# Layer-norm roots taken with a token to a partition, and the router's logits and ranks, in a two-block transformer

## What is computed

```python
def layer_norm_2(x, g, b):
    mu = jnp.mean(xf, -1, keepdims=True)
    var = jnp.mean(jnp.square(xf - mu), -1, keepdims=True)
    return ((xf - mu) * lax.rsqrt(var + LN_EPS)).astype(x.dtype) * g + b

def routed_moe(x, router_w, router_b, w_gate, w_up, w_down):
    aff = jax.nn.sigmoid((xt @ router_w).astype(jnp.float32))      # 256 tokens x 16 experts
    sel = aff + router_b
    # best of 4 groups of 4 experts by the sum of its two best sel; in it the two best experts
    # weights: their aff, divided by the sum of both
    ...
for l in range(2):
    x = layer_norm_2(ALPHA * x + mixer(x), ln_g[l, 0], ln_b[l, 0])
    x = layer_norm_2(ALPHA * x + routed_moe(x, ...), ln_g[l, 1], ln_b[l, 1])
```

## Time and profile before

| | |
|---|---|
| median of 3 runs | 2592.41 us (2579.9 to 2612.1) |
| the profiled execution | 2592.51 us |
| its span, first to last instruction | 2590.7 us |
| mean granted TensorE clock over the span | 0.953 of full |

### The profile page before, as it was taken

One profiled execution on the slowest core, in us unless ns is written; L12 is line 12 of the kernel. 1 busy time (PEld: TensorE's weight loads), 2 busy tenths in 40 slices (PEclk: granted clock), 3 DMA queues, 4 the chain that ended last, 5 costly groups with the idle time before them and its releaser, 6 DMA issues.

```text
span 2590.7 us, 34009 instructions
## 1 busy us (share of the span) xinstructions
PE 2452.1 (95%) x14244; PEld 2102.6 (81%) x14244; DVE 1719.2 (66%) x2263; ACT 1194.5 (46%) x1520; POOL 98.7 (4%) x187
## 2 busy tenths in 40 slices
PE   5999999899999999999999998989999899899998
PEld 1788888767789999998899997867777787778776
DVE  5897776652656656655556655568878775688786
ACT  3222212333434444445444444456656644566665
POOL 0111111010000000000000000000000000000000
PEclk8999999998869999999899998999999896999999
DMA  6677887322114554455334452238877630388774
GB/s 257 216 243 255 267 265 260 131 76 95 66 35 161 179 195 163 175 193 217 139 131 164 178 203 99 82 128 332 333 270 297 252 114 33 114 330 321 287 301 181
DMA packets 80387, 501.19 MB, mean 193 GB/s; under 512 B 9604, under 2 KB 10708, under 8 KB 28496
## 3 DMA queue, kind: packets, MB, share of 16 engines
q1 hardware_dynamic: 59120, 423.66, 44.4%
q0 software_dynamic: 21088, 75.01, 9.1%
HBM read 497.58 MB, written 1.05 MB: 192 GB/s over the span
## 4 chain that ended last, share of the span: by engine, by line
PE 69%; DVE 16%; ACT 9%; issue 3%; DMA 2%; DVEq 0%; ACTq 0%; SPq 0%; POOL 0%; POOLq 0%
PE bank L394 67%; DVE wl L1913 7%; ACT wh L1304 6%; DVE macc L1949 2%; ACT s L1394 1%; DVE f L2074 1%; PE bank L577 1%; DMA raw<-in_wstream 1%; DVE s L2065 1%; DMA raw<-in_wmod 1%; PE bank L1198 1%; DVE rs L1973 1%; DVE hl L2049 1%; ACT H L1403 0%; DVE tmp L2042 0%
## 5 line engine op out<-in xcount | busy, mean ns | idle before, releaser
L1913 DVE TENSOR_TENSOR wl<-raw,wh 128x2048 fp32r<-128x2048 f32 (+1 forms) x430 | 903.8, 2107 | 404.7 <-ACT wh L1304 402.1
L1304 ACT ACTIVATE wh<-raw 128x2048 fp32r<-128x2048 f32 (+1 forms) x430 | 755.0, 1763 | 366.4 <-PE bank L394 354.3
L394 PE MATMUL bank<-hh,wh 128*128 128x258 f32 (+2 forms) x2200 | 700.8, 319 | 43.9 <-DVE wl L1913 23.5
L394 PE MATMUL bank<-hh,wl 128*128 128x258 f32 (+2 forms) x2200 | 681.5, 310 | 0.0
L394 PE MATMUL bank<-hl,wh 128*128 128x258 f32 (+2 forms) x2200 | 680.1, 309 | 0.0
L394 PEld LDWEIGHTS bank<-hh,wh 128*128 128x128 f32 x2200 | 428.1, 195 | 72.3 <-issue 23.0
L394 PEld LDWEIGHTS bank<-hl,wh 128*128 128x128 f32 x2200 | 429.0, 195 | 18.5
L394 PEld LDWEIGHTS bank<-hh,wl 128*128 128x128 f32 x2200 | 427.4, 194 | 19.2
L394 PE MATMUL bank<-wh,hh 128*128 128x512 f32 (+1 forms) x704 | 278.4, 395 | 5.5 <-DVE hl L2825 2.8
L394 PE MATMUL bank<-wl,hh 128*128 128x512 f32 (+1 forms) x704 | 274.0, 389 | 0.0
L394 PE MATMUL bank<-wh,hl 128*128 128x512 f32 (+1 forms) x704 | 274.0, 389 | 0.0
(11 more groups left out here) (424 smaller groups left out, 2716.8 us busy)
## 6 DMA issues: line engine op xcount, KB each, us to landing
raw<-in_wstream SPq DMA_DIRECT2D x393, 1024.0 KB, 5.0
mring<-in_wmod POOLq DMA_DIRECT2D x128, 512.0 KB, 4.6
raw<-in_wmod SPq DMA_DIRECT2D x8, 1024.0 KB, 9.1
X<-in_xT SPq DMA_DIRECT2D x1, 2048.0 KB, 12.3
bias<-in_nabias POOLq DMA_DIRECT2D x16, 128.0 KB, 2.5
c_sglg<-in_sglg POOLq DMA_DIRECT2D x1, 1024.0 KB, 5.2
c_sglb<-in_sglb POOLq DMA_DIRECT2D x1, 1024.0 KB, 7.5
out<-X SPq DMA_DIRECT2D x4, 256.0 KB, 2.2
```

The lines of the kernel that those rows point to most:

```text
L394: return e.matmul(out, lhsT, rhs, start=start, stop=stop, skip_group_check=True)
L1304: e.activation(wh[i % NB][:, o], raw[i % NR][:, o], ACT.Copy).then_inc(*slab_high(st.split + m))
L1913: e.tensor_tensor(wl[i % NB][:, o], raw[i % NR][:, o], wh[i % NB][:, o].bitcast(F32), ALU.subtract).then_inc(*slab_low(st.split + m))
```

## The change

1. Layer norms: the squares are summed with the squares as the stationary operand and one column of `ones` as the moving one: 16 products of one column, which leave a token's sum in its own partition, 128 x 2. Scale and epsilon, square root and reciprocal then work on 128 x 2. VectorE multiplies the identity by the roots (128 x 256 into `rs`), and one more product of `ones` with this diagonal spreads them to all partitions in PSUM, from where the scaling reads them.
2. For layer norms 0 and 2 ScalarE loads the table of the sigmoid by a small activation right behind the square root.
3. Router: `X` is now the stationary operand and the router's weights (16 columns) the moving one: 16 products, two a chunk. The logits come out as 128 x 32; the two transposes and the copy fall away.
4. Ranks: TensorE waits for "group" instead of "gates". VectorE does the weights of the experts behind the ranks, the flag and the two `Pm` tiles of group 0; the other six `Pm` tiles are written two at a time inside groups 0 to 2, behind the copy of the gates' values (`gG`).

```diff
         def layer_norm(i):
             st.kept.remove(bank_of["sum", i])
-            square_sums(7 + i, T)
+            b = bank(("ssq", 7 + i), dve_out, "mean", 7 + i)
+            for k in range(KC):
+                w.wait_ge(act_out, "square", 7 + i, k)
+                for c in range(2):
+                    ins = mm(b[:, c:c + 1], sq4[:, k % 4, P * c:P * c + P], ones[:, 0:1], k == 0 and c == 0, k == KC - 1)
+                ins.then_inc(*result("ssq", 7 + i, k))
+            b = bank(("ln root", i), dve_out, "scaled", 7 + i, KC - 1)
+            w.wait_ge(dve_out, "diag", 7 + i)
+            mm(b[:, 0:T], ones[:], rs[:, 0:T], True, True).then_inc(*result("ln root", i))
...
-                ins = mm(b[0:16, 0:T], q.rw[:, k, :], X[:, k, 0:T], k == 0, k == KC - 1)
+                for s_ in range(2):
+                    ins = mm(b[:, 16 * s_:16 * s_ + 16], X[:, k, P * s_:P * s_ + P], q.rw[:, k, :], k == 0 and s_ == 0, k == KC - 1)
             ins.then_inc(*result("aff", l))
-            b = bank(("aff t", l), dve_out, "aff t", l)
-            w.wait_ge(act_out, "aff", l)
-            for s_ in range(2):
-                ins = e.transpose(b[:, 16 * s_:16 * s_ + 16], q.rows[:, P * s_:P * s_ + P], ident[0:16, 0:16])
-            ins.then_inc(*result("aff t", l))
...
-            w.wait_ge(dve_out, "gates", l)
+            w.wait_ge(dve_out, "group", l)
...
-            root(7 + i, T)
+            w.wait_ge(dve_out, "mean", 7 + i)
+            e.activation(rt[:, 0:2], rt[:, 0:2], ACT.Sqrt).then_inc(*act_out("root", 7 + i))
+            if i % 2 == 0:
+                act(warm[:], ones[:, 0:1], ACT.Sigmoid, key=("sigmoid", i))
...
-            inv_root(7 + i, T, 1.0 / D, 1e-5)
+            e.tensor_scalar(rt[:, 0:2], banks[bank_of["ssq", 7 + i]][:, 0:2], 1.0 / D, 1e-5, ALU.mult, ALU.add).then_inc(*dve_out("mean", 7 + i))
+            w.wait_ge(act_out, "root", 7 + i)
+            e.reciprocal(rt[:, 0:2], rt[:, 0:2]).then_inc(*dve_out("inverse", 7 + i))
+            e.tensor_tensor(rs[:, 0:T].rearrange("p (b t) -> p b t", b=2), bc(ident[:], 2), rt[:, 0:2].unsqueeze(2).to_broadcast([P, 2, P]),
+                            ALU.mult).then_inc(*dve_out("diag", 7 + i))
...
+            places(0)
+            behind()
+            step(e.memset(q.top[:, :, 2:8], -4 * BIG), "two")
...
                 e.tensor_copy(q.gG[:, 0:S, :], banks[bank_of["ge", l, g]][:, 0:4 * S].rearrange("p (s x) -> p s x", x=4)).then_inc(*dve_out("ge", l, g))
+                if g < 3:
+                    places(g + 1)
```

More of the change, by code:

```diff
@@ L156, in program @@
     rs = sb(ctx, "rs", [P, 512])
+    rt = sb(ctx, "rt", [P, 4])
     sq4 = sq[:].rearrange("p a (b t) -> p (a b) t", t=T)
@@ L294, in moe_room @@
             q.top = sb(ph, f"top{l}", [P, 2, 8])
-            q.rows = sb(ph, f"aff{l}", [16, T])
             q.sm = sb(ph, f"sm{l}", [P, 8, 2])
@@ L678, in layer_norm @@
             st.kept.remove(bank_of["sum", i])
-            square_sums(7 + i, T)
+            b = bank(("ssq", 7 + i), dve_out, "mean", 7 + i)
+            w.wait_ge(dve_out, "ones")
+            for k in range(KC):
[6 more added lines that the diff above has]
+            mm(b[:, 0:T], ones[:], rs[:, 0:T], True, True).then_inc(*result("ln root", i))
         def mixer0():
@@ L1167, in group @@
                 b = small(("ge", l, g), dve_out, "ge", l, g)
+                w.wait_ge(dve_out, "gates", l)
                 for s_, c in blocks:
@@ L1801, in moe @@
             w.wait_ge(result, *before)
-            e.activation(q.rows[:], banks[bank_of["aff", l]][0:16, 0:T], ACT.Sigmoid).then_inc(*act_out("aff", l))
+            e.activation(q.R[0][:], banks[bank_of["aff", l]][:, 0:32].rearrange("p (q x) -> p q x", q=2), ACT.Sigmoid).then_inc(*act_out("aff", l))
             for s_ in range(2):
@@ L2461, in scaled_parts @@
                 if k < KC:
-                    w.wait_ge(dve_out, "rs", nm, 0)
-                    e.scalar_tensor_tensor(X[:, k, 0:T], X[:, k, 0:T], g[:, k:k + 1], rs[:, 0:T], ALU.mult,
+                    e.scalar_tensor_tensor(X[:, k, 0:T], X[:, k, 0:T], g[:, k:k + 1], banks[bank_of["ln root", nm - 7]][:, 0:T], ALU.mult,
                                            ALU.mult).then_inc(*dve_out("scaled", nm, k))
@@ L2476, in layer_norm @@
             dve_out.mark("centred", i)
-            inv_root(7 + i, T, 1.0 / D, 1e-5)
+            w.wait_ge(result, "ssq", 7 + i, KC - 1)
+            e.tensor_scalar(rt[:, 0:2], banks[bank_of["ssq", 7 + i]][:, 0:2], 1.0 / D, 1e-5, ALU.mult, ALU.add).then_inc(*dve_out("mean", 7 + i))
[4 more added lines that the diff above has]
+                            ALU.mult).then_inc(*dve_out("diag", 7 + i))
             w.wait_ge(const_in["lng"], 0)
+            w.wait_ge(result, "ln root", i)
             scaled_parts(7 + i, lng[:, i, :], parts)
@@ L2746, in moe @@
             w.wait_ge(result, *before)
-            w.wait_ge(result, "aff t", l)
-            e.tensor_copy(aff[:], banks[bank_of["aff t", l]][:, 0:32].rearrange("p (q x) -> p q x", q=2)).then_inc(*dve_out("aff t", l))
+            w.wait_ge(act_out, "aff", l)
             w.wait_ge(const_in[f"rb{l}"], 0)
-            behind()
             step(e.tensor_tensor(sl[:], aff[:], bc(q.rb[:], 2), ALU.add), "sel")
@@ L2770, in moe @@
             step(e.tensor_tensor(dst, tmp, q.sm[:, 1, :].unsqueeze(2).to_broadcast([P, 2, 4]), ALU.is_equal), "group")
+            dve_out.mark("group", l)
             behind()
@@ L2778, in moe, with places @@
                 step(e.max(q.top[:, t, :], m1[:, t, :]), "top", t)
+            b = banks[bank_of["rank", l]]
+            w.wait_ge(result, "rank", l)
+            behind()
+            step(e.tensor_copy(q.rank[:], b[:, 0:8].rearrange("p (q g) -> p q g", q=2)), "rank")
+            behind()
+            e.tensor_scalar(q.flag[:], b[0:1, 8:12], 128.0, None, ALU.is_gt).then_inc(*dve_out("flag", l))
+            w.wait_ge(const_in[f"iota{l}"], 0)
+            behind()
+            def places(g):
+                for t in range(2):
+                    e.tensor_scalar(q.Pm[:, g, t, :], q.iota[:], q.rank[:, t, g:g + 1], one[:, t, g:g + 1],
+                                    ALU.is_equal, ALU.mult).then_inc(*dve_out("pm", l, g))
+            places(0)
             behind()
@@ L2793, in moe @@
             e.tensor_tensor(gt[:], gt[:], q.sm[:, 3, :].unsqueeze(2).to_broadcast([P, 2, 16]), ALU.mult).then_inc(*dve_out("gates", l))
[L2794 to L2805, removed]
             def scatter(g, b0):
```

## The result

The changed kernel takes 2617.31 us (median of four executions, 2610.34 to 2625.32) against 2586.15 of the kernel before: a ratio of 1.0115, 95% interval 1.0069 to 1.0162. The prediction was 2596.0 with a range of 2575 to 2610; the result is outside of it. It is less than 2% and so within the "same" that the prediction was nearly sure of, but it is a real slowdown, and eight times the 3.8 us that the sum gave.

What follows compares the result with a forecast made beforehand. The prediction took the serial chain of small steps in norms and routers, with nothing running beside it, as the bound. Layer norms +3.1 and routers +0.7 us on 2592.5 gave 2596.3, told as 2596, range 2575 to 2610.

Steps and rivals of the forecast that it cites:

- the sum: Whole kernel: layer norms +3.1 us and routers +0.7 us, together +3.8 us on the profiled 2592.5 us.
- squares: Sum of squares in each layer norm: 3.72 us becomes 5.06, +1.34, with the clock falling behind the first 20 records.
- mean to scaling: Small steps in each layer norm: 2.77 us becomes 2.21 at half clock, a gain of 0.56.
- scaling from PSUM: Layer norm scaling reads roots from PSUM: costed at nothing; a tenth of its pace would be 0.3 us a norm.
- logits: Router logits, twice: 5.30 us before, 7.1 after at half clock, +1.82 each.
- logits' end to ranks: Router, twice: 5.43 us becomes 3.5, with 16 transposes at half clock ending last, -1.93 each.
- ranks: Ten rank records in each router: 1.84 us becomes 2.28 at half clock, +0.44 each.
- gather: Gather behind the ranks: already mostly at half clock, so unchanged at 5.66 us.
- moved VectorE work: Experts' weights beside the gather, six Pm tiles in groups 0 to 2: hidden; 4.0 us if the cover were gone.
- the likeliest case: Clock falls within the squares and stays down to the gather: 2596 us, chance 0.45.
- The clock comes back: Rival: clock rises within the router's logits after 3.2 us at half; 2588.6 us, chance 0.15.
- Cold from the first square: Slower rival: clock falls before the sum of squares begins, gather cold to its end; +15, 2607.5 us, chance 0.15.

Runs made afterwards that it cites:

- e10: Kernel before with only the ranks beside the choice of experts and the moved places; norms, logits and banks as they were: ratio 1.0105.
- e3: Changed kernel with norm 1's product with the diagonal written to the bank of its own sums, so later banks stand as before: 2587.99 us, ratio 1.0001.
- e1: The kernel before, unchanged, run once more as a control: ratio 1.0018.
- e12: Changed kernel, banks still turned, with nine unread 128x256 products ahead of the odd attention: 2589.71 us, ratio 1.0032.
- e15: Whole change plus unread fill products ahead of the odd attention and late in it, against the kernel before: 2582.55 us, ratio 1.0005.
- e17: Kernel before with the ranks' part alone and fills ahead of the odd attention, late in it and ahead of the last turns of Y: ratio 0.9977.
- e18: Kernel before with 16 unread products late in the odd attention, the same program as e9 timed a second time: ratio 0.9984.
- e9: Kernel before with 16 unread 128x256 products late in the odd attention, first timing: ratio 0.9945.
- e16: Kernel before with the 16 unread products late in the odd attention and five more ahead of the last turns of Y: ratio 0.9935.

## Why the prediction was wrong

*What was right.* The chain of small steps, by its own terms, in the profiled execution of the changed kernel:

| step | predicted | measured |
|---|---|---|
| squares | 5.06 | 5.35, 5.20, 5.59 and 5.96 in the four norms |
| mean to scaling | 2.21 | 2.45, then 2.37 three times |
| scaling from PSUM | no dearer than 3.26 | 3.22 |
| logits | 7.1 | 6.98 |
| logits' end to ranks | 3.5, behind the transposes | 3.11, behind the transposes |
| ranks | 2.28 | 1.18 (clock up again) |
| gather | 5.66 | 5.44 |
| moved VectorE work | hidden | no cost beyond the spread (groups of e10 330.3, before 328.2 and 331.0) |

The clock fell inside the squares and stayed down through the logits, as the likeliest case had it. From centring to the first product with the gates that makes 28.02 us against 28.28 before, where the sum said +1.1: the ranks ran at full clock. Norm 2 with its router makes -0.2, norms 1 and 3, squares to scaling, +1.2 and +1.9: by its own terms the sum would have been about +2.6 in place of +3.8, because the squares lost more and the routers came out better. (In "The clock comes back" the prediction prices the full-clock ranks at -0.3, elsewhere at -0.6; that is 0.6 us over two routers and changes nothing.) With the banks put right (e3) the whole change is worth 1.0001, and the 3.8 us of the sum lie within that interval.

*The step that failed.* The sentence "So what the chain gains or loses the kernel gains or loses in full" and the sum built on it, which covered only the norms and routers. Everything behind them was costed at nothing, and the odd mixer behind norm 1 is where 28.5 us came from. The diff shows a claimed bank in place of none, and the prediction counted the product that fills it (0.70 to 1.05 us) but not what the claim moves: each later result, until the fixed banks of the attention. The wait that this adds is small (0.83 us at the first logit, 0.55 us more idle time in all); what it sets off is not. The prediction had in hand that the half clock can last through an attention with TensorE busy (34.58 of 35 us) but did not ask what had put it there, and what would make that come earlier.

*The rivals.* Three of the four were about the clock inside the norm and the router, and none looked further. "Cold from the first square", the one on the slower side, is near the total (2607.5) by accident; its mechanism did not happen, for the clock fell in the squares and not ahead of them, and was up again for the ranks. That the +2.0 to +8.6 us in the groups behind router 0 come from the change is not shown: e3, with every part of it, had 360.03 us there, e1 359.31.

## What to carry to other kernels

Where results go round a ring of banks, one more claim moves every later result: compare the bank of each result before and after, up to the next place with fixed banks, and look who now waits for whose drain. Where TensorE works in small products, look at the few tenths of a microsecond that it idles, since they can help to decide at which clock the next hundred microseconds run; cost a changed wait there with the clock's fall as an outcome (here up to 28 us for 0.5). Put the landmarks of two profiles side by side before explaining anything, and run the kernel before again: it shows which stretches repeat.

## What the runs showed of the hardware

- A fall of the clock can last. TensorE was busy for 105.1 of 106 us at 0.50, with products of 64 to 256 columns, many of them only 32 or 64 rows deep, among weight products of 128 rows and 256 columns. The same work with nine wide products in place of the waits ahead of it ran 33 us longer at full clock (e12).
- The same program is not always on the same side. With the head of the attention filled, 1 of 58 executions took over 2600 us (e12 to e15 and e17); filled only late, 4 of 12 in e18, but 0 of 12 in e9, the same program, and 1 of 12 in e16.
- One-column squares cost nothing more than wide ones as long as the clock is up. In e12, norm 2:

```profile
2194.73 3.73 PE L394 MATMUL bank<-ones,sq 128*128 128x1 f32 x32 [0.96 <-ACT sq L1352]
```

That is 3.73 us for 32 records against 3.72 for the wide form; the 1.5 to 2.2 us more that they took in the four norms of the changed kernel go with the clock's fall inside them.
